# One inference step of a hybrid encoder: the router's logits are formed inside the products that turn the frames

## What is computed

```python
def _moe_ffn(x, g, router, w1, w3, w2):
    h = _rmsnorm(x, g).reshape(-1, D)
    logits = (h @ router).astype(jnp.float32)
    top_v, top_i = lax.top_k(logits, TOP_K)          # 2 of 8 experts
    gates = jax.nn.softmax(top_v, axis=-1)
    e_flat = top_i.reshape(-1)
    order = jnp.argsort(e_flat)
    tok = order // TOP_K
    xs = h[tok]                                      # frames sorted by expert
    sizes = jnp.bincount(e_flat, length=N_EXPERTS)
    a = lax.ragged_dot(xs, w1, sizes)
    b = lax.ragged_dot(xs, w3, sizes)
    y = lax.ragged_dot(jax.nn.silu(a) * b, w2, sizes)
    ...
    return x + out.reshape(B, T, D)
```

## Time and profile before

| | |
|---|---|
| median of three runs | 4518.84 us (4516.87 to 4525.02) |
| the profiled execution, its own time | 4524.06 us |
| its span | 4522.5 us |
| TensorE busy | 4216.5 us, 93% of the span |
| TensorE weight loads busy | 4034.7 us, 89% |
| VectorE, ScalarE, GpSimd busy | 2106.3, 1614.2, 898.1 us (47%, 36%, 20%) |
| mean granted clock of TensorE | 0.964 |
| HBM read, written | 493.67 MB, 95.72 MB |

### The profile page before, as it was taken

How to read it: one execution, slowest core, us unless ns; L and a number is a source line. 1 busy time by engine, 2 the same in 40 slices (tenths; PEclk the granted TensorE clock), 3 DMA queues, 4 the chain that set the end, 5 groups by cost and what they waited for, 6 DMA issues and landing times. The chain is left out here.

```text
span 4522.5 us, 84835 instructions
## 1 busy us (share of the span) xinstructions
PE 4216.5 (93%) x33666; PEld 4034.7 (89%) x33666; DVE 2106.3 (47%) x2822; ACT 1614.2 (36%) x2845; POOL 898.1 (20%) x657
## 2 busy tenths in 40 slices
PE   6999998998999999899888887999999999999992
PEld 4999997887989999899875786999999999999992
DVE  3555565765441111343336534444454545545554
ACT  3772332555210000221115323534343444444441
POOL 0334211442433323243211222000000000000001
PEclk8999999999999999999989987999999999999996
DMA  2223587665432222342200125556565666666675
GB/s 72 72 86 101 147 220 197 154 163 164 138 87 88 81 87 78 122 134 81 52 20 0 39 74 128 159 153 170 165 176 168 178 176 188 175 182 193 181 207 185
DMA packets 999020, 592.68 MB, mean 131 GB/s; under 512 B 114961, under 2 KB 957298, under 8 KB 998818
## 3 DMA queue, kind: packets, MB, share of 16 engines
q1 hardware_dynamic: 923824, 510.20, 40.7%
q10 hardware_dynamic: 65970, 52.44, 3.9%
q0 software_dynamic: 9024, 27.24, 1.9%
HBM read 493.67 MB, written 95.72 MB: 130 GB/s over the span
## 5 line engine op out<-in xcount | busy, mean ns | idle before, releaser
L2578 DVE TENSOR_TENSOR experts_w<-experts_raw,experts_w 128x1024 fp32r<-128x1024 f32 x352 | 415.4, 1222 | 139.1 <-ACT experts_w L2542 139.1
L210 PE MATMUL experts_pa<-experts_hx,experts_w 128*128 128x264 f32 (+6 forms) x1408 | 411.7, 292 | 2.9 <-DVE experts_w L2578 2.9
L210 PE MATMUL experts_pd<-experts_hid,experts_w 128*128 128x264 f32 (+6 forms) x1408 | 410.0, 291 | 0.0
L212 PE MATMUL experts_pa<-experts_hx,experts_w 128*128 128x264 f32 (+6 forms) x1408 | 409.0, 290 | 0.0
L211 PE MATMUL experts_pa<-experts_hx,experts_w 128*128 128x264 f32 (+6 forms) x1408 | 408.7, 290 | 0.0
L210 PE MATMUL experts_pb<-experts_hx,experts_w 128*128 128x264 f32 (+6 forms) x1408 | 408.7, 290 | 0.0
L211 PE MATMUL experts_pd<-experts_hid,experts_w 128*128 128x264 f32 (+6 forms) x1408 | 408.4, 290 | 0.0
L212 PE MATMUL experts_pd<-experts_hid,experts_w 128*128 128x264 f32 (+6 forms) x1408 | 408.1, 290 | 0.0
L212 PE MATMUL experts_pb<-experts_hx,experts_w 128*128 128x264 f32 (+6 forms) x1408 | 408.0, 290 | 0.0
L211 PE MATMUL experts_pb<-experts_hx,experts_w 128*128 128x264 f32 (+6 forms) x1408 | 407.6, 289 | 0.0
L210 PE MATMUL proj_pm<-hT,proj_w_hi 128*128 128x384 f32 (+1 forms) x1152 | 388.2, 337 | 0.0
(11 more groups left out here) (440 smaller groups left out, 10661.3 us busy)
## 6 DMA issues: line engine op xcount, KB each, us to landing
experts_raw<-in_moe_w SPq DMA_DIRECT2D x352, 512.0 KB, 4.7
experts_raw<-in_moe_w SPq DMA_DIRECT2D x128, 704.0 KB, 5.9
projected<-proj_out SPq DMA_DIRECT2D x48, 544.0 KB, 4.0
proj_w<-in_gdn_w_in ACTq DMA_DIRECT2D x48, 512.0 KB, 4.1
ffnup_w<-in_ffn_w SPq DMA_DIRECT2D x44, 512.0 KB, 5.0
ffndown_w<-in_ffn_w SPq DMA_DIRECT2D x32, 704.0 KB, 4.8
mixout_w<-in_gdn_w_out SPq DMA_DIRECT2D x32, 512.0 KB, 3.9
hidden<-ffnup_hid ACTq DMA_DIRECT2D x22, 544.0 KB, 2.8
```

The costliest lines, as they stand in the source:

```text
L210: pe.matmul(out, as_r(w_hi), as_r(x_hi), start=first, stop=False)
L212: return pe.matmul(out, as_r(w_lo), as_r(x_hi), start=False, stop=last)
L2578: dve.tensor_tensor(as_r(w[:, u, 1, x, 0:KD, :]), raw[:, x, u, 0:KD, :], w[:, u, 0, x, 0:KD, :], ALU.subtract).then_inc(split[x][u], 1)
```

## The change

It touches `route_stage` alone.

- A buffer `turn` holds, for each slab, 128 columns of the identity and the router's eight columns. GpSimd copies the identity into it, VectorE writes the scaled router as before. One plain product with 136 columns per slab replaces the eight-column product and the transpose. Slabs go in groups of three, three and two to a PSUM bank, two tiles deep.
- ScalarE copies the 128 turned columns of each group (27 copies instead of 18, up to 384 columns wide). Behind each copy VectorE sums the group's eight-column pieces over its slabs into `part`; at the end it sums the three groups and multiplies by `rtok`.
- There are three row buffers instead of two.
- VectorE no longer waits for the exponential before the slots: the gates' instructions stand at its end of the stage.
- `chosen` is three tiles; the first expert's list is made, copied and gathered tile by tile.
- Three rows of filler are added: two `keep_busy` products behind the lengths, seven behind the counts, six behind the list.

```diff
+TURN = P + NE
+K_GROUPS = ((0, 1, 2), (3, 4, 5), (6, 7))
+ROWS = 3
...
-        chosen = st.sb("chosen", [P, NT, FIRST_CAP])
+        chosen = [st.sb(f"chosen{i}", [P, NT, n]) for i, (c, n) in enumerate(job_tiles(FIRST_CAP))]
...
-        ph = st.ps("ph", [P, 4, 4, P])
+        ph = st.ps("ph", [P, 2, len(K_GROUPS), 512])
...
             def _(pool):
+                pool.tensor_copy(turn[:, :, 0:P], m["const"][:, 0:P].unsqueeze(1).broadcast_to([P, KD, P])).then_inc(ident_set, 1)
                 pool.memset(zero[:, :], 0).then_inc(zero_set, 1)
...
-                pool.wait_ge(ids_ready, PRE + 1)
                 for i, (s, n) in enumerate(job_tiles(FIRST_CAP)):
+                    pool.wait_ge(ids_ready, PRE + i + 1)
                     pool.indirect_dma_start(out=r["rows"][0:n, i, :], out_offset=None, in_=m["h_dram"],
...
                 last.then_inc(summed, 1)
+                keep_busy(pe, m, ph[:, 0, 0, :], 2)
+                pe.wait_ge(ident_set, PRE + 1)
                 pe.wait_ge(w_ready, PRE + 1)
                 for t, (s, n) in enumerate(TILES):
-                    for k in range(KD):
-                        last = pe.matmul(pl[0:n, t, :], xT[:, k, s:s + n], wr[:, k, :], start=(k == 0), stop=(k == KD - 1))
...
-                        if i >= 4:
-                            pe.wait_ge(h_copied, PRE + i - 3)
-                        for k in range(4):
-                            last = pe.transpose(ph[0:n, i % 4, k, :], xT[:, 4 * h + k, s:s + n], m["const"][:, 0:P])
+                    for b, ks in enumerate(K_GROUPS):
+                        if t >= 2:
+                            pe.wait_ge(part_taken, PRE + fills(t - 2, b) + 1)
+                        for g, k in enumerate(ks):
+                            last = pe.matmul(ph[0:n, t % 2, b, TURN * g:TURN * (g + 1)], xT[:, k, s:s + n], turn[:, k, :], start=True, stop=True)
                         last.then_inc(turned, 1)
...
-                pe.wait_ge(chosen_ready, PRE + 1)
-                pe.wait_ge(rooted, PRE + 1)
+                pe.wait_ge(h_copied, PRE + fills(NT, 0))
+                keep_busy(pe, m, ph[:, 0, 0, :], 7)
                 for i, (c, rows) in enumerate(job_tiles(FIRST_CAP)):
+                    pe.wait_ge(chosen_ready, PRE + i + 1)
                     for t, (s, n) in enumerate(TILES):
-                        last = pe.matmul(pid[0:rows, i:i + 1], chosen[0:n, t, c:c + rows], idsf[0:n, t:t + 1], start=(t == 0), stop=(t == NT - 1))
-                last.then_inc(ids_summed, 1)
+                        last = pe.matmul(pid(i, rows), chosen[i][0:n, t, :], idsf[0:n, t:t + 1], start=(t == 0), stop=(t == NT - 1))
+                    last.then_inc(ids_summed, 1)
+                keep_busy(pe, m, ph[:, 0, 0, :], 6)
...
-                dve.tensor_tensor(lg[:, 0:NT - 1, :], pl[:, 0:NT - 1, :], rtok[:, 0:NT - 1].unsqueeze(2).broadcast_to([P, NT - 1, NE]), ALU.mult)
...
+                for t in range(NT):
+                    n = TILES[t][1]
+                    for b in range(len(K_GROUPS)):
+                        dve.wait_ge(h_copied, PRE + fills(t, b) + 1)
+                        last = dve.tensor_reduce(part[0:n, t, b, :], turned_group(t, b)[0:n, :, P:TURN].rearrange("p k e -> p e k"), AX.X, ALU.add)
+                        if (t, b) < (NT - 1, len(K_GROUPS) - 1):
+                            last.then_inc(part_taken, 1)
+                v(last)
+                v(dve.tensor_reduce(lg[:, :, :], part[:, :, :, :].rearrange("p t b e -> p t e b"), AX.X, ALU.add))
+                v(dve.tensor_tensor(lg[:, :, :], lg[:, :, :], rtok[:, :].unsqueeze(2).broadcast_to([P, NT, NE]), ALU.mult))
```

More of the change, by code:

```diff
@@ L2119, in route_stage @@
         zero = st.sb("zero", [P, TABLE // P], I32)
-        pl, prank, ptot = (st.ps(n, [P, NT, NE]) for n in ("logits", "rank_in_tile", "tile_total"))
-        ph = st.ps("ph", [P, 4, 4, P])
-        psmall = st.ps("small", [P, NT + 3])
-        pss, pid = psmall[:, 0:NT], psmall[:, NT:NT + 3]
+        ph = st.ps("ph", [P, 2, len(K_GROUPS), 512])
+        pcount, pss = st.ps("counts", [P, 2, NT, NE]), st.ps("lengths", [P, NT])
+        prank, ptot = pcount[:, 0, :, :], pcount[:, 1, :, :]
+        turned_group = lambda t, b: ph[:, t % 2, b, 0:TURN * len(K_GROUPS[b])].rearrange("p (k c) -> p k c", c=TURN)
+        pid = lambda i, n: ph[0:n, 1, i, 0:1]
+        fills = lambda t, b: len(K_GROUPS) * t + b
         w_ready, summed, rooted, inverted, numbers_l = (st.sem(n) for n in ("w_ready", "summed", "rooted", "inverted", "numbers_loaded"))
@@ L2126, in route_stage @@
         xT, root, rtok = m["xT"], r["root"], r["rtok"]
-        proj, vs, es, counted, ranked = (st.sem(n) for n in ("projected", "vector_step", "exped", "counted", "ranked"))
-        turned, h_copied = st.sem("turned"), st.sem("h_copied")
-        h_stored = [st.sem(f"h_stored{u}") for u in range(2)]
+        vs, es, counted, ranked, gap_ready = (st.sem(n) for n in ("vector_step", "exped", "counted", "ranked", "gap_ready"))
+        turned, h_copied, part_taken, ident_set = (st.sem(n) for n in ("turned", "h_copied", "logits_taken", "ident_set"))
+        h_stored = [st.sem(f"h_stored{u}") for u in range(ROWS)]
         ids_set, slots_ready = st.sem("ids_set"), st.sem("slots_ready")
@@ L2151, in _ @@
                 pool.wait_ge(ids_set, PRE + NT)
-                pool.wait_ge(h_stored[0], PRE + 16 * ((NT + 1) // 2))
-                pool.wait_ge(h_stored[1], PRE + 16 * (NT // 2))
-                pool.wait_ge(ids_ready, PRE + 1)
+                for u in range(ROWS):
+                    pool.wait_ge(h_stored[u], PRE + 16 * (NT // ROWS))
                 for i, (s, n) in enumerate(job_tiles(FIRST_CAP)):
+                    pool.wait_ge(ids_ready, PRE + i + 1)
                     pool.indirect_dma_start(out=r["rows"][0:n, i, :], out_offset=None, in_=m["h_dram"],
@@ L2194, in _ @@
                 act.wait_ge(inverted, PRE + 1)
-                for i in range(2 * NT):
-                    t, h = i // 2, i % 2
+                for t in range(NT):
                     n = TILES[t][1]
[L2198 to L2202, removed]
+                    if t >= ROWS:
+                        act.wait_ge(h_stored[t % ROWS], PRE + 16 * (t // ROWS))
+                    for b, ks in enumerate(K_GROUPS):
+                        act.wait_ge(turned, PRE + fills(t, b) + 1)
+                        act.activation(hrow[0:n, t % ROWS, ks[0] * P:(ks[-1] + 1) * P].rearrange("p (k c) -> p k c", c=P), turned_group(t, b)[0:n, :, 0:P],
+                                       ACT.Copy, scale=rtok[0:n, t:t + 1]).then_inc(h_copied, 1)
+                act.wait_ge(gap_ready, PRE + 1)
                 act.activation(e21[:, :], m2[:, :], ACT.Exp).then_inc(es, 1)
```

57 lines of the change are left out of this document (27 added, 30 removed).

## The result

The kernel with the change took 4492.38 us (median of four runs, 4485.36 to 4493.11) beside 4521.61 us for the kernel before in the same session: a ratio of 0.9933, 95% interval 0.9915 to 0.995. It is faster by 29.2 us; 30.5 were forecast. The time itself was forecast as 4488.3 us, reckoned from the median of 4518.84 that was known then.

The account below looks back on a forecast made before the run. It saw one chain through the route stage as the bound, with VectorE waiting 16.53 us for the exponential. Experts beginning 27.5 us earlier plus 3.0 from their filler gave 30.5: 4518.84 - 30.5 = 4488.3 us, range 4480 to 4502.

Parts of the forecast that it names:

- eleven one-column rows: Lengths' rows in the 1 us clock window of 2664 before the change: 0.09 to 0.10 us each.
- the bounds of -4.8 and +5.7: Sizes of the forecast case: list warm as well, 4483.5 us; experts' filler and last filler cold, 4494 us.
- Turning: Route stage's 72 products of 136 columns on TensorE: six rows cold, 138 warm, 1.4 + 15.9 us, ending at 2686.9.
- The plain product against the transpose: Per slab in the turning: 0.23 us plain against at most 0.15 for a transpose, about 1.5 times its TensorE time.
- a factor of four: Rival in the turning: a plain product costs four transposes, 43.2 us instead of 17.3; 4.6 us less, 4514.2; chance 3%.
- A clock that stays low: Rival in the turning: the clock never rises, turning takes 32.7 us; 8.4 us less, 4510.4; chance 6%.
- Load and product in series: Slower rival in the turning: loads not beside products, 0.43 us a cold row; 20.8 us slower, 4539.6; chance 5%.
- The tail: From the last turning product through copy, sums and multiplication to the choice: choice starts at 2688.6, against 2695.90.
- What is late next is the logits themselves: Between choice and slots on VectorE: the 16.53 us of waiting are gone, slots start at 2693.3 against 2717.01.
- The list: First expert's list on TensorE, taken cold: 10.2 us, ending at 2714.4; warm it would be 5.4 us.
- The end of the stage: Route stage's close: TensorE's filler 2721.9, GpSimd's drain 2721.2, VectorE 2719.4; experts begin at 2723.7 instead of 2751.2, 27.5 us less.
- Experts' filler: Filler at the experts' start, at the upper clock: 3.4 us instead of 6.60; with what follows, 3.0 us less.

Follow-up runs that it names:

- The run with one wait: The change, but with GpSimd waiting for the whole list before the first of its three gathers, as in the kernel before: 4500.95 us.

## Why the prediction was right

Its times of the new chain stood within 0.6 us of the trace throughout:

| step | forecast | measured |
|---|---|---|
| end of the lengths | 2666.20 | 2666.55 |
| turning starts, ends | 2669.6, 2686.9 | 2670.12, 2687.37 |
| choice starts | 2688.6 | 2688.82 |
| slots start | 2693.3 | 2693.65 |
| `chosen` starts | 2702.9 | 2703.26 |
| list starts, ends | 2704.2, 2714.4 | 2704.68, 2714.80 |
| filler behind the list ends | 2721.9 | 2721.97 |
| experts' filler starts, takes | 2723.7, 3.4 | 2723.65, 3.67 |

The sums and the readings of the prediction hold, but for these. The "eleven one-column rows" of the window of 2664 are all that reach into it: the rows of the lengths start every 0.11 us, not 0.09 to 0.10, and the 203 and 189 ns a row are means of 0.21 us for loads of 128 columns and 0.11 for loads of 64. And the bounds of -4.8 and +5.7, widened by 2 and 6, give 4481.5 to 4500; the range went 1.5 to 2 us beyond them. The result hangs on neither.

- *Turning.* The pitch taken from the 144-column rows of another stage, scaled by columns and by the clock, gave 17.3 us; 17.25 were measured. The clock was put at 4.8 us after the filler's start and came some 4 after it. So close a hit is in part luck: in five kernels with the filler ahead of it and the 136-column products it took 16.99 to 17.80 us, by when the clock rose. That dense 136-column products raise the clock was argued from the transposes; the kernel without the first filler shows it.
- *The plain product against the transpose.* The price of 0.23 us a slab held. Against the transpose it is 1.5 times only by the upper bound of 0.15, which has the waits at the banks in it; within a bank the trace has the transposes start every 0.11 us, so it is nearer two. The Trainium skill, "TensorE: Matmul & The Clock Gate", Terms, speaks of a factor of four; the measured rows disagree, as the prediction had read.
- *The rivals.* A clock that stays low would have shown rows of 0.23 us to the end; they came every 0.116 from 2671 on. Load and product in series, the slower rival, needed 0.285 us and more a row; the loads lie under the products (1.00 us busy for both in the window of 2671). The same page, "What overlaps and what doesn't", would have it otherwise where the row groups agree, and this trace is against it again.
- *The tail.* "What is late next is the logits themselves" is what VectorE's rows show: its only wait between choice and slots is 1.32 us for the counts. The terms of this tail (0.3, 0.45, 0.3, 0.4 and 0.3 us) were estimates without rows of their own; together they are 1.75 us, and from the last product's end to the choice it took 1.45.
- *The list.* It was taken at the lower clock, and in the change the clock fell 0.1 us after it began (0.89 in the window of 2704). In four other kernels it fell later, and the filler behind the list took the difference. So the sum of the two, 17.3 us in all six kernels with both, was safe, and that 10.2 us for the list alone came out was luck.
- *The end of the stage.* TensorE's filler last by a little, GpSimd close behind it: 2722.0 and 2719.6. The drain of GpSimd ended 4.3 us after the last gather's issue (2715.26), inside the bound of 5.6. The run with one wait shows what hung on it: 4 us.
- *Experts' filler.* 3.67 us for 3.4, and nothing behind it was late. ScalarE waits 1.6 us twice for the experts' weights now, which it did not before; VectorE's split still sets the first product, 11.00 us after the start. By then the clock has fallen again, before as now (0.50 in the window of 2764 before, of 2733 now), so the warm clock shortens the filler and no product of the experts.

What the prediction did not see is small. It counted the fillers as given and costed their places right, but did not ask what each is worth: the first costs some 2 us, the one behind the counts shortens the list in some runs but not the stretch, and the one behind the list loses 2.45 us of start and gets 1.7 back. Nor did it say that the move of the gates, worth 5.5 us of the stretch in the kernel before, is worth nothing once the sweep is one. Both lie inside the sum, which is why the sum held.

The median fell by 29.2 us and the profiled execution by 30.95, around the forecast of 30.5. The profiled stage accounts for 30.83 of the 30.95, so nothing was given back later.

## What to carry to other kernels

When TensorE goes twice over the same weights, once for a few columns, look at the clock of the narrow sweep: paced by its loads it ran here at half speed for its whole length. Put its columns into the wide sweep, at the price of a plain product in place of a transpose (0.23 us a slab here), or at least its products between the wide ones. Cost a move by the wait that takes its place, and test two moves that shorten the same wait apart, for their gains don't add (between choice and slots 6.0 us by the one, and 16.3 by both and by the other alone). Filler pays as far as something else holds the stage's end nearly as long (here the landing of the last gather), so find out what that is before adding any.

## What the runs showed that I had not expected

- *Narrow products and the clock.* TensorE was shown busy all through the 29.28 us of eight-column products, and the clock stayed at the lower level. The same products between transposes ran for 20 us at the upper level. So the busy share of a stretch does not tell its clock. The Trainium skill, "TensorE: Matmul & The Clock Gate", Part 4, says that transposes do not bring the upper clock; in the kernel before, it rose 3.7 us into a stretch of nothing but transposes.
- *The gap that loses the clock.* Behind filler that had been at the upper level, a gap of 1.67 us kept it and one of 3.49 lost it early in the next filler, at a price of 1.7 us. The length of the gap alone does not part the cases: without the first filler the clock outlived a gap of 3.87 us and fell 1.4 us into the list, and in the change it fell 2.9 us after the filler behind the counts had ended.
- *When the clock rises* varies between runs of the same stage, from 3 to 6 us after dense work begins, and moves the turning by 1.5 us (18.54 and 20.00).
- *Gathers from GpSimd* that were issued 1.3 us apart took at most 5.4 to 6.3 us to land in the five kernels that have them so, and those 2 to 3.3 us apart at most 4.3 to 4.5 in the other seven: spread gathers and a short drain behind the last went together in all twelve.
- *What paces narrow products* is their loads. In the logits of the kernel before, the rows start every 0.213 us where a load has 128 columns, and every 0.107 in the last tile of frames, where it has 64, at the same granted clock. The windows ahead of that tile and in it, and the transposes that follow:

```profile
2692.00:2693.00 1.00, 1.00 (x6) 1.00 (x6) 0.00 (x0) 0.00 (x0) 0.00 (x0) 0.50 0.00 0
...
2694.00:2695.00 1.00, 1.00 (x11) 1.00 (x11) 0.00 (x0) 0.00 (x0) 0.00 (x0) 0.50 0.00 0
```

```profile
2695.41 5.49 PE L2176 MATMUL route_ph<-const,xT 128*128 128x128 f32 x32
```
